# Sub-layer borders in token halves: two groups begin with tokens 0 to 255, the group before ends with tokens 256 to 511

## The reference

```python
for i in range(DEPTH):                               # DEPTH = 2
    hn = rms_norm(h, gains[0])
    mix = retention(hn, ...) if i % 2 == 0 else gated_deltanet(hn, ...)
    h = h + rms_norm(mix, gains[1])
    ff = sq_relu_mlp(rms_norm(h, gains[2]), mlp_w_up[i], mlp_w_down[i])   # square(relu(h @ up)) @ down, 1024 -> 4096 -> 1024
    h = h + rms_norm(ff, gains[3])
```

## Time and profile before

| | |
|---|---|
| median of 3 runs | 1629.2 us (1629.11 to 1631.49) |
| span of the profiled execution | 1626.2 us |
| PE busy | 1506.0 us, 93% |
| DVE, ACT, POOL busy | 699.1, 539.7, 619.8 us |

### The profile page before, as it was taken

How to read it: one execution, slowest core, us unless ns; L and a number is a source line. 1 busy time by engine, 2 the same in 40 slices (tenths; PEclk the granted TensorE clock), 3 DMA queues, 4 the chain that set the end, 5 groups by cost and what they waited for, 6 DMA issues and landing times.

```text
span 1626.2 us, 19219 instructions
## 1 busy us (share of the span) xinstructions
PE 1506.0 (93%) x7393; PEld 1260.4 (78%) x7393; DVE 699.1 (43%) x1218; ACT 539.7 (33%) x916; POOL 619.8 (38%) x276
## 2 busy tenths in 40 slices
PE   6999999989889999999979799948998899999997
PEld 6888888568778888888768688738986788888886
DVE  3650021762464200440465689974657542013323
ACT  4322333242333222232234556336324322223221
POOL 3544434104424443444424333215323244344442
PEclk9999999999999999999989999969999999999999
DMA  5332233202213223232212212201002132332231
GB/s 213 104 103 84 97 103 103 78 1 97 86 56 121 85 102 104 79 102 104 78 58 78 78 55 79 75 1 53 27 0 79 65 106 102 104 102 81 102 104 52
DMA packets 66505, 134.25 MB, mean 83 GB/s; under 512 B 3616, under 2 KB 3968, under 8 KB 66176
## 3 DMA queue, kind: packets, MB, share of 16 engines
q1 hardware_dynamic: 64016, 125.90, 23.6%
q10 hardware_dynamic: 2416, 7.33, 1.3%
HBM read 131.13 MB, written 2.10 MB: 82 GB/s over the span
## 4 chain that ended last, share of the span: by engine, by line
PE 51%; issue 27%; DVE 11%; POOL 9%; ACT 1%; DMA 0%; POOLq 0%; ACTq 0%; DVEq 0%
PE bank L360 15%; PE bank L361 15%; PE bank L362 15%; POOL w_lo L285 9%; DVE tmp L1569 2%; DVE gq L1469 1%; DVE block_x L1571 1%; PE bank L705 1%; PE bank L604 1%; PE bank L610 1%; PE bank L714 1%; DVE block_l L1559 0%; DVE k_grown L1616 0%; DVE gq L1467 0%; PE bank L560 0%
## 5 line engine op out<-in xcount | busy, mean ns | idle before, releaser
L285 POOL TENSOR_TENSOR w_lo<-w_raw,w_hi 128x1024 fp32r<-128x1024 f32 x232 | 567.8, 2469 | 828.7 <-ACT w_hi L821 828.7
L821 ACT ACTIVATE w_hi<-w_raw 128x1024 fp32r<-128x1024 f32 x232 | 232.9, 1053 | 531.5 <-PE bank L362 503.6
L360 PE MATMUL bank<-act_hi,w_hi 128*128 128x512 f32 (+1 forms) x960 | 351.5, 366 | 10.0 <-DVE act_lo L1285 9.2
L361 PE MATMUL bank<-act_lo,w_hi 128*128 128x512 f32 (+1 forms) x960 | 348.7, 363 | 0.0
L362 PE MATMUL bank<-act_hi,w_lo 128*128 128x512 f32 (+1 forms) x960 | 348.7, 363 | 0.0
L360 PEld LDWEIGHTS bank<-act_hi,w_hi 128*128 128x128 f32 x960 | 183.8, 191 | 39.1 <-DVE act_lo L1285 10.3
L362 PEld LDWEIGHTS bank<-act_hi,w_lo 128*128 128x128 f32 x960 | 183.4, 191 | 27.6
L361 PEld LDWEIGHTS bank<-act_lo,w_hi 128*128 128x128 f32 x960 | 183.8, 191 | 27.1
L361 PE MATMUL bank<-w_lo,hid_hi 128*128 128x512 f32 x512 | 202.5, 395 | 0.0
L360 PE MATMUL bank<-w_hi,hid_hi 128*128 128x512 f32 x512 | 201.6, 394 | 0.0
L1389 DVE TENSOR_TENSOR relu_sq<-relu 128x512 f32<-128x512 f32 x64 | 51.0, 798 | 347.2 <-ACT relu L838 346.5
(11 more groups left out here) (239 smaller groups left out, 1857.4 us busy)
## 6 DMA issues: line engine op xcount, KB each, us to landing
w_raw<-in_mlp_w_up_dram SPq DMA_DIRECT2D x32, 1024.0 KB, 5.5
w_raw<-in_mlp_w_down_dram SPq DMA_DIRECT2D x32, 1024.0 KB, 5.0
w_raw<-in_ret_w_in_dram SPq DMA_DIRECT2D x24, 1024.0 KB, 5.2
w_raw<-in_gdn_w_in_dram SPq DMA_DIRECT2D x16, 1024.0 KB, 5.3
w_raw<-in_ret_w_out_dram SPq DMA_DIRECT2D x8, 1024.0 KB, 5.0
gains<-in_norm_gains_dram ACTq DMA_DIRECT2D x8, 512.0 KB, 4.7
w_raw<-in_gdn_w_out_dram SPq DMA_DIRECT2D x4, 1024.0 KB, 5.1
resid<-in_x_dram SPq DMA_DIRECT2D x4, 512.0 KB, 9.3
```

Source lines behind the costliest of these rows:

```text
L285: nc.gpsimd.tensor_tensor(w_lo[:, s, kt, :], w_raw[:, s, kt, :], w_hi[:, s, kt, :].bitcast(F32), ALU.subtract).then_inc(w_ready, 1)
L360: pe.matmul(dst, sta_hi, mov_hi, start=first, stop=False)
L361: pe.matmul(dst, sta_hi, mov_lo, start=False, stop=False)
L821: act.activation(w_hi[:, slot, kt, :], w_raw[:, slot, kt, :], ACT.Copy).then_inc(w_high, 1)
```

## The change

Weights get four more slots, `side_hi` and `side_lo`, laid over tiles of the MLP's and the mixers' buffers that are free at that time; `HI` and `LO` list all six. Four things then change, and one small one with them.

1. `tail` takes the place of `last_group` at b=1, b=2 and at the end: chunk 0 for all four token tiles, then chunks 1 to 3 for tiles 0 and 1, then chunks 1 to 3 for tiles 2 and 3. The transposes of tiles 0 and 1 stand together ahead of the last two parts. At b=3 (two chunks) `last_group` keeps its order.
2. `begin` covers two groups: tokens 0 to 255 of the first (8 parts of 256 columns), transposes of tile 2, tokens 0 to 255 of the second with the transposes of tile 3 after its fourth part, then tokens 256 to 511 of both. Its four chunks stand in four slots.
3. The transposes of tiles 2 and 3 go to the right halves of banks 0 to 3, which the token halves leave free until then; copies out of them come in four pieces of 128 x 256 for two of 128 x 512.
4. In `norms` ACT splits the four head chunks: the first now behind the second `norm_share`, the third and fourth around `resid_root` of tile 3, ahead of `high_acts` of tiles 2 and 3.
5. On one column, `inv_root` has five instructions: the tensor_tensor ones become tensor_scalar with operands read from memory.

In the DeltaNet the beta and a product is cut in halves too, and its small transposes move between the two late pieces of the first group.

```diff
+    TAIL_SLOTS = (0, 1, 0, 2)
+    HEAD_SLOTS = [(0, 1, 4, 5), (0, 1, 3, 4), (0, 1, 3, 4), (0, 1, 4, 5)]
...
+            def tail(norm, start, a_hi, a_lo):
...
+                pe.wait_ge(emptied, 4 * g0)
+                for m in range(4):
+                    one(m, 0)
+                for j in range(1, 4):
+                    one(0, j)
+                    one(1, j)
...
+                for j in range(1, 4):
+                    if j == 3:
+                        turn_tile(norm, 0)
+                        turn_tile(norm, 1)
+                    one(2, j)
+                    one(3, j)
...
-            def begin(b, between=None):
+            def begin(b, between=None, within=None):
...
                 for j in range(2):
                     for m in range(4):
-                        part(c, j, 0, 2, m, True, act_hi, act_lo, slice(0, 2 * P), fresh=m == 0)
-                        if (j, m) == (1, 0):
-                            turn_tile(b, 2)
-                        if (j, m) == (1, 1):
-                            turn_tile(b, 3)
+                        part(c, j, 0, 2, m, True, act_hi, act_lo, early, fresh=m == 0, slot=slots[j])
+                turn_tile(b, 2)
+                if b:
+                    pe.wait_ge(emptied, 4 * NEXT_GROUP[b])
+                for j in range(2):
+                    for m in range(4):
+                        part(c + 2, j, 1, 2, m, True, act_hi, act_lo, early, fresh=m == 0, slot=slots[2 + j])
+                    if j == 0:
+                        turn_tile(b, 3)
                 pe.wait_ge(sem("act_low"), 2 * TT * (b + 1))
...
+                for g in range(2):
+                    for j in range(2):
+                        for m in range(4):
+                            done = part(c + 2 * g, j, g, 2, m, True, act_hi, act_lo, late, slot=slots[2 * g + j])
...
                 norm_share(b, 1)
-                if not before:
-                    act.wait_ge(w_landed[0], 16)
-                    high(0)
+                if b:
+                    act.wait_ge(chunk_used, ready)
+                head_splits(b, 0, 1)
                 high_acts(b, 0)
                 high_acts(b, 1)
                 mix_root(b, 2)
-                splits(after, 0, 2, 1, 1)
+                if b == 3:
+                    act.wait_ge(bank_full, 4 * NEXT_GROUP[b])
+                head_splits(b, 1, 2)
                 mix_root(b, 3)
                 resid_root(b, 2)
+                if b == 2:
+                    act.wait_ge(bank_full, 4 * NEXT_GROUP[b])
+                head_splits(b, 2, 3)
                 resid_root(b, 3)
+                head_splits(b, 3, 4)
                 high_acts(b, 2)
                 high_acts(b, 3)
...
                 link(dve.reciprocal(t[1], root))
+                if x.shape[-1] == 1:
+                    link(dve.tensor_scalar(t[2], t[0], t[1], t[1], ALU.mult, ALU.mult))
+                    link(dve.tensor_scalar(t[2], t[2], -0.5, 1.5, ALU.mult, ALU.add))
+                    return dve.tensor_scalar(out_, t[2], t[1], None, ALU.mult)
```

More of the change, by code:

```diff
@@ L279, in _, with low_part @@
         def _(pool):
-            def low_part(s, before):
+            def low_part(raw, before, slot):
                 for half in range(2):
@@ L887, in high_acts, with head_splits, third_split, norms @@
                 act.wait_ge(sem("acts_transposed"), TT * b + m + 1)
-                for half in range(2):
-                    act.activation(act_hi[:, 4 * half:4 * half + 4, m * P:(m + 1) * P],
-                                   tall(bank[2 * m + half]), ACT.Copy).then_inc(sem("act_high"), 1)
-            def norms(b, before, after):
+                for first, n, src in turned_pieces(m):
+                    done = act.activation(act_hi[:, first:first + n, m * P:(m + 1) * P], src, ACT.Copy)
+                    if (first + n) % 4 == 0:
+                        done.then_inc(sem("act_high"), 1)
+            def head_splits(b, first, last):
+                c = FIRST_CHUNK[b]
+                for j in range(first, last):
+                    split_one(c + j, HEAD_SLOTS[b][j])
+            def third_split(start):
+                g0, c0, u0 = start
+                act.wait_ge(chunk_used, u0 + 1)
+                split_one(c0 + 4, 0)
+            def norms(b, ready):
                 mix_root(b, 0)
@@ L975, in _, with up_group @@
             half_squares(1)
-            splits(RET_OUT, 1, 4, first=2, last=3)
-            norms(1, (RET_OUT, 1, 4, 4, 4), MLP[0][0][0])
+            tail_splits(RET_OUT)
+            norms(1, RET_OUT[2] + 3 + 3)
             def mlp(layer):
-                def up_group(i, p, first=1):
-                    splits(up, i, 2, first)
+                def up_group(i, p):
+                    if half or isinstance(i, int) and i > 2:
+                        splits(up, i, 2)
+                    elif i == 1:
+                        act.wait_ge(bank_full, 4 * up[0] + 4)
+                        split_one(up[1] + 5, 1)
+                    elif i == 2:
+                        splits(up, i, 2, first=2)
                     for m in range(4):
@@ L1028, in _ @@
             act.wait_ge(sem("ba_full"), 1)
-            act.activation(ba_t[:, :], bank[4][:, :], ACT.Copy).then_inc(sem("ba_out"), 1)
+            for half in range(2):
+                act.activation(ba_t[:, 2 * half * P:2 * (half + 1) * P], bank[4 + half][:, 2 * P:T], ACT.Copy)\
+                    .then_inc(sem("ba_out"), 1)
             order = [(GDN_K, gk), (GDN_V, gv), (GDN_Q, gq)]
@@ L1281, in low_acts @@
             def low_acts(b, m):
-                for half in range(2):
-                    dve.wait_ge(sem("act_high"), 2 * (TT * b + m) + half + 1)
-                    where = (slice(None), slice(4 * half, 4 * half + 4), slice(m * P, (m + 1) * P))
-                    dve.tensor_tensor(act_lo[where], tall(bank[2 * m + half]), act_hi[where].bitcast(F32),
-                                      ALU.subtract).then_inc(sem("act_low"), 1)
+                for first, n, src in turned_pieces(m):
+                    if first % 4 == 0:
+                        dve.wait_ge(sem("act_high"), 2 * (TT * b + m) + first // 4 + 1)
+                    where = (slice(None), slice(first, first + n), slice(m * P, (m + 1) * P))
+                    done = dve.tensor_tensor(act_lo[where], src, act_hi[where].bitcast(F32), ALU.subtract)
+                    if (first + n) % 4 == 0:
+                        done.then_inc(sem("act_low"), 1)
             def norms(b, more=False):
```

226 lines of the change are left out of this document (144 added, 82 removed).

## The result

The changed kernel takes 1586.8 us (median of 4 runs, 1586.04 to 1588.95) against 1629.15 for the kernel before, measured beside it. The ratio is 0.9741, with a 95% interval of 0.9727 to 0.9755: about 42 us less, where 32.5 were forecast. The profiled execution has a span of 1584.2 us, 42.0 less than before.

The account below looks back on a forecast made before the run. PE, busy 93% of the span, was taken as the bound, with its idle time at the borders. Terms +1.2 - 14 - 10 - 8.5 - 1 - 0.2 = -32.5 against 1629.2 gave 1597 us, range 1588 to 1613.

Parts of the forecast that it names:

- b=1: Border b=1: PE's gaps mostly covered, residual idle 2.9 us, of a border cost of 17.75; taken as -14 us.
- b=2: Border b=2 and DeltaNet: two of POOL's three subtractions leave the convolutions, 4.2 us each; taken as -10 us in all.
- b=3: Border b=3, two chunks, old order: residual idle 7.4 us, overhead 1.2, clock drop 0.7; -8.5 us, final chain -0.2.
- What bounds: Whole kernel: PE busy 93% of the span; a border costs 17.75 us, three of them 53 us.
- The first gap: PE idle 5.80 us before tile 0's transposes at b=1; 4.1 us of tile 0's chain is waiting for POOL.
- start and group norms: Start of launch: second group in halves costs +1.2 us; group norms: shorter roots give -1 us.
- k's start: In the DeltaNet behind b=2: k's first group is full about 2 us earlier.
- rival 1: DeltaNet keeps its length, POOL's subtractions still in the convolutions: b=2 gives 2, 1605 us; 15 in 100.
- rival 2: Clock still drops at every border, 2.9 us each: 1605 us, or 1602 at b=1 and b=3 alone; 12 in 100.
- rival 3: Roots still wait for POOL, about 1.2 us twice and 2.2 once per border, half hidden: 1601 us; 8 in 100.
- rival 4: ACT's order delays tile 3's transposes behind chunk 3's split; at 10 us per border, four borders: 1637 us; 4 in 100.

Follow-up runs that it names:

- the three moves together: Changed kernel with silu of heads 4 to 7 before the split, heads 0 to 3 between k copies, b=3's tile 0 copies early: 1588.2 us.
- the other probe: Changed kernel plus six POOL subtractions beside DVE tensor_scalar on 128 x 1, 3, 31, 127, 511, 2 values; ran once, time says nothing.

## Why the prediction was wrong

**What bounds, and the start.** Both stand. The first gap's 4.1 us of waiting roots is confirmed by the kernel with the roots alone: 5.80 us became 1.26. The forecast for start and group norms was +0.2 in all, and +0.06 was measured; the two terms by themselves can't be told from the shift between executions. The matmul behind the group norms starts at 346.84 in the change, and anywhere from 345.97 to 347.78 in five of the experiments, which are the same kernel up to there. The measured terms of the table, from one execution of each kernel, are good to about 1 us for the same reason.

**b=1: right** (-14, measured -15.25). Residual idle was 1.86 and not 2.9, and the granted clock is 1.00 in the windows from 442.3 to 462.4.

**b=2: the step that failed.** The prediction says "of three subtractions the last is left, under `convolve(1)`", so two go, at 4.2 us each, and I took -10 against a measured -15.45. All three went. The chunk of the last one can be split only when PE is through with the first v chunk, and that was not before 875.37:

```profile
875.37 2.01 ACT L899 ACTIVATE w_hi<-w_raw 128x1024 fp32r<-128x1024 f32 x2 [3.33 <-PE bank L402]
```

DVE, two subtractions shorter, was then nearly through (its stretch ends at 877.1, and POOL's subtraction starts at 876.51). I had counted subtractions by their old place and not by where DVE would be once the first two were gone. The experiment with POOL's extra work shows both directions: two put back draw the third in, 24.7 us become 36.8, and the idle time at the attention matrices ends at 1053.22, 10.8 us later than in the change. The rest of the miss is k's start. Before, the convolutions begin at 872.91; 15.19 less, for what was gained up to there, is 857.72. They begin at 852.42, so 5.3 us earlier, where I had about 2. And about 2 us of the sum of 5.3 and 12.2 are not used: from the end of the stretch to PE's second turn of k there were 4.3 us and are 6.3, since PE waits for ACT there (the 2.16 at 883.35). Why k starts earlier is read from the traces and not tried. The last matmul of k's first group starts at 863.91 before and at 845.57 now, 3.2 us earlier than the 15.19 alone would give; the residual gaps at b=2 are 1.20 + 0.46 + 0.46 + 0.52, where I had 3.2 and 1.3. From there to the first convolution it took 9.0 us and takes 6.9, and one difference is that ACT now copies k's tiles one by one as they fill, where it had copied all four at the end (865.00 to 867.08).

**b=3: right in kind, 2.7 us too small** (-8.7 with the end, measured -11.4). The gap before tile 2's transposes was to be 2.7 and is 0.59; the first was to be 0.4 and is nothing; 3.15 before the first matmul was foreseen as 3.5. The low clock behind it cost more than I had: about 3.4 us of work at half rate, 1.7 us, for my 0.7.

**The rivals.** The DeltaNet did not keep its length (rival 1). The clock does not drop at b=1 and b=2, but at b=3 it does (rival 2 in part): 0.54 and 0.50 behind the gap of 3.15, high again from 1221. My measure for it, that 3.94 us was the shortest gap with a low clock behind it, was too long: it fell behind 2.01 us in the kernel with the roots alone, and in the DeltaNet of the change behind 4.01 and 2.16 us (0.50 from 866.2 to 868 and from 883.3 to 885).

```profile
1217.60:1219.00 1.40, 1.33 (x6) 1.33 (x7) 1.29 (x7) 1.40 (x2) 1.30 (x2) 0.54 0.00 0
1219.00:1221.00 2.00, 2.00 (x11) 2.00 (x11) 1.97 (x2) 1.30 (x4) 2.00 (x2) 0.50 0.56 109
1221.00:1223.00 2.00, 2.00 (x19) 2.00 (x18) 2.00 (x2) 0.00 (x0) 2.00 (x1) 0.97 0.97 369
```

The roots don't wait (rival 3), but its price was far off: I charged "about 1.2 us twice and 2.2 once per border, half of it hidden". At three borders that makes 1604, not the 1601 I wrote, and the kernel in which they wait takes 1620.5. With tensor_tensor on the roots it is 8.74 us of idle time before tile 2 alone, and 34 us in all. I had followed tile 0's chain and never asked what POOL does beside tile 2 once four chunks are split for a border. ACT's order (rival 4) cost nothing: PE waits for `side_lo` 0.46 us per border.

**The range.** Its lower end was added up wrong: 1597 less the 3.5 and the 2 that I named is 1591.5, not 1589.

**Still open:** what decides whether the clock falls. It fell behind 3.15 us at b=3 and not behind 3.17 us at b=1 in the kernel with the old tail order; it fell behind the 2.01 us of the kernel with the roots alone and not behind the 3.22 us at 17.40 in the change, where the window 17.4 to 19 has 1.00. The length of the gap alone doesn't decide it, and no run here tells what does.

## What to carry to other kernels

Where two engines hold each other up, what one gives away is worth more than its own waits: count who will be beside whom after the first savings, since each wait removed can move the next one out of reach, and each one added can draw another in. Ask of every tiny DVE instruction on a critical chain what POOL does beside it: here one operand form, the same arithmetic, decided 21 us in one order of work and 34 in another. And once a chain behind is saturated (the DVE chain of the DeltaNet), taking idle time of PE away ahead of it moves the idle time and nothing else: the silu moved ahead gave nothing, and neither did the three moves together.

## What the runs showed of the hardware

A DVE tensor_scalar on 128 x 1 values runs at its own 0.15 us beside a subtraction of POOL, and with operands read from memory it takes 0.21 to 0.28; on 128 x 2, 3 and 31 it waits, and so does a tensor_tensor on 128 x 1 (2.07 to 2.28 us). The wait need not end with POOL's current instruction: it took 11.86 us while POOL ran instructions without a pause between them, where the same kind got in after one of them (2.29 us) in the other probe. The Trainium skill, "SBUF — State Buffer", section "SBUF: two separate sides", lets whoever comes first keep the pair of ports that VectorE and GpSimd share for its whole instruction. The trace shows such waits, and longer ones than one instruction.
